# Alternating turns and unit products inside a score step of a two-layer attention trunk

## What is computed

```python
for l in range(DEPTH):                       # DEPTH = 2
    h = rms_norm(x, norm_g[l])
    proj = jnp.einsum('btd,dc->btc', h, w_in[l])
    q_a, kv_a, g_a, z_a, q_b, k_b, v_b, f_b, z_b, merge = jnp.split(proj, split_at, axis=-1)
    y_a = nsa_mixer(q_a, kv_a, g_a, ...) * jax.nn.silu(z_a)
    y_b = fox_mixer(q_b, k_b, v_b, f_b, b_forget[l]) * jax.nn.silu(z_b)
    merged = (jax.nn.sigmoid(r_a) * jnp.einsum('btc,cd->btd', y_a, w_proj_nsa[l])
              + jax.nn.sigmoid(r_b) * jnp.einsum('btc,cd->btd', y_b, w_proj_fox[l]))
    x = x + jnp.einsum('btd,de->bte', merged, w_out[l])
```

## Time and profile before

| | us |
|---|---|
| median of 3 runs | 1454.97 (1454.9 to 1455.04) |
| span of the profiled execution | 1452.2 |
| TensorE busy in it | 1443.0 (99%) |
| DVE, ACT, POOL busy | 1050.6, 915.4, 469.1 |
| attention of the two layers, about | 72 to 515 and 788 to 1230 |
| one inner cycle | 56.1 |

### The profile page before, as it was taken

One profiled execution on the slowest core, in us unless ns is written; L12 is line 12 of the kernel. 1 busy time (PEld: TensorE's weight loads), 2 busy tenths in 40 slices (PEclk: granted clock), 3 DMA queues, 4 the chain that ended last, 5 costly groups with the idle time before them and its releaser, 6 DMA issues.

```text
span 1452.2 us, 24707 instructions
## 1 busy us (share of the span) xinstructions
PE 1443.0 (99%) x7550; PEld 1223.2 (84%) x7550; DVE 1050.6 (72%) x2422; ACT 915.4 (63%) x1904; POOL 469.1 (32%) x578
## 2 busy tenths in 40 slices
PE   9999999999999999999999999999999999999998
PEld 7888888888888888888888888888888888888887
DVE  6888888888888864444578888888888887643444
ACT  6677777777877752223365877877877876522234
POOL 2435535445445310000023345445445453000000
PEclk9999999999999999999999999999999999999999
DMA  9221222222222143333453222222222212433332
GB/s 285 75 69 49 59 58 58 59 56 51 55 58 59 46 144 97 91 101 93 110 183 83 57 54 59 58 59 59 59 58 55 61 44 59 145 95 102 92 102 91
DMA packets 213890, 117.97 MB, mean 81 GB/s; under 512 B 9304, under 2 KB 212272, under 8 KB 213296
## 3 DMA queue, kind: packets, MB, share of 16 engines
q1 hardware_dynamic: 211408, 107.49, 27.2%
q0 software_dynamic: 1728, 8.66, 1.6%
q10 hardware_dynamic: 672, 0.83, 0.2%
HBM read 110.54 MB, written 6.42 MB: 81 GB/s over the span
## 4 chain that ended last, share of the span: by engine, by line
PE 98%; DVE 1%; issue 0%; ACT 0%; POOL 0%; DVEq 0%; POOLq 0%; ACTq 0%
PE acc L1814 69%; PE turned L1889 8%; PE o_pair L1914 7%; PE scores L1874 4%; PE scores L1876 4%; PE turned L2056 1%; PE misc L1933 1%; PE o_pair L1922 1%; PE scores L1814 1%; PE misc L1837 1%; PE o_pair L1948 1%; PE acc L2171 0%; PE o_pair L2171 0%; PE o_pair L2073 0%; PE scores L1992 0%
## 5 line engine op out<-in xcount | busy, mean ns | idle before, releaser
L1814 PE MATMUL acc<-u_hi,w_hi 128*128 128x512 f32 x1096 | 433.4, 395 | 0.0
L1814 PE MATMUL acc<-u_lo,w_hi 128*128 128x512 f32 x1096 | 430.9, 393 | 0.0
L1814 PE MATMUL acc<-u_hi,w_lo 128*128 128x512 f32 x1096 | 428.3, 393 | 0.0
L936 ACT ACTIVATE prob<-prob,row_max 128x384 f32<-128x384 f32 (+3 forms) x384 | 215.5, 561 | 143.2 <-DVE row_max L1400 140.8
L1217 DVE TENSOR_TENSOR w_lo<-w_raw,w_hi 128x1024 fp32r<-128x1024 f32 x184 | 230.7, 1254 | 83.1 <-ACT w_hi L807 82.4
L730 POOL TENSOR_SCALAR prob<-prob,row_inv,gates 128x256 f32<-128x256 f32 (+3 forms) x256 | 168.2, 657 | 302.8 <-DVE row_inv L1407 302.0
L807 ACT ACTIVATE w_hi<-w_raw 128x1024 fp32r<-128x1024 f32 x184 | 193.6, 1053 | 87.7 <-PE acc L1814 82.9
L1814 PEld LDWEIGHTS acc<-u_hi,w_hi 128*128 128x128 f32 x1096 | 206.4, 188 | 39.1 <-issue 0.2
L1814 PEld LDWEIGHTS acc<-u_lo,w_hi 128*128 128x128 f32 x1096 | 206.0, 188 | 37.0 <-issue 0.2
L1814 PEld LDWEIGHTS acc<-u_hi,w_lo 128*128 128x128 f32 x1096 | 206.4, 188 | 36.3
L1400 DVE CUSTOM_DVE_ANT_0 prob<-scores,causal 128x384 f32<-128x384 f32 (+3 forms) x384 | 185.7, 484 | 45.0 <-PE scores L1876 34.1
(11 more groups left out here) (276 smaller groups left out, 2346.1 us busy)
## 6 DMA issues: line engine op xcount, KB each, us to landing
w_raw<-in_w_in_dram SPq DMA_DIRECT2D x140, 512.0 KB, 3.7
w_raw<-in_w_proj_nsa_dram SPq DMA_DIRECT2D x16, 512.0 KB, 3.6
w_raw<-in_w_proj_fox_dram SPq DMA_DIRECT2D x16, 512.0 KB, 3.6
w_raw<-in_w_out_dram SPq DMA_DIRECT2D x16, 512.0 KB, 3.7
x_scratch<-xT POOLq DMA_DIRECT2D x2, 2048.0 KB, 9.2
xT<-x_scratch POOLq DMA_DIRECT2D x2, 2048.0 KB, 8.3
x_nat<-in_x_dram SPq DMA_DIRECT2D x4, 512.0 KB, 6.7
c_w<-in_cmp_w_k_dram SPq DMA_DIRECT2D x4, 512.0 KB, 6.1
```

What stands on the lines that cost most here:

```text
L936: act.activation(prob[:, ring, 0:width], prob[:, ring, 0:width], ACT.Exp, bias=row_max[:, ring:ring + 1], scale=-1.0, accum_out=row_sum[:, ...
L1814: ins = pe.matmul((bank or acc[par])[0:width, :], own_w, rhs, start=(n == 0), stop=(n == 23))
```

## The change

Between two turns of a step one product of the unit that is running is issued, if the slot still has one to issue. Where a narrow value product stands behind the first turn already, none is put there. The number of products at the end of each slot stays as it was.

```diff
-                def turn_step(pair, s, scored=None, ended=None):
+                def turn_step(pair, s, scored=None, ended=None, between=None):
...
                         if kt == 0 and ended:
                             value_narrow(*ended, 1)
+                        elif kt < qt:
+                            between()
...
+                def one_unit_product():
+
+                    nonlocal done
+                    if done < (plan.cum[s] if s < plan.slots else done):
+                        u = done // 24
+                        unit_piece(done - 24 * u, done - 24 * u + 1, *cycle.unit(u), free=bank_read(cycle, u))
+                        done += 1
+
...
-                        turn_step(*cycle.step(s - LAG_TURN), scored=scored if narrow else None, ended=ended_at(s))
+                        turn_step(*cycle.step(s - LAG_TURN), scored=scored if narrow else None, ended=ended_at(s),
+                                  between=one_unit_product)
```

## The result

| | before | changed |
|---|---|---|
| median (lowest to highest), us | 1454.93 (1454.84 to 1455.04) | 1465.55 (1464.99 to 1465.79) |
| profiled execution: its time, its span, us | not recorded, 1452.2 | 1465.69, 1464.0 |

The ratio is 1.0075, with a 95% interval of 1.0063 to 1.0086: slower by 10.6 us. The forecast was 1464.9. The spans of the two profiled executions differ by 11.8, about 1 us more than the medians: before, the median lies 2.8 above the span of the profile, in the changed kernel 1.6. What follows takes distances within an execution, which don't depend on that.

What follows compares the result with a forecast made beforehand. TensorE, busy 1443.0 of 1452.2 us, was taken as the bound, so only instruction costs and its waits matter. Late last turn 8.3 plus small costs 1.6 gave 9.9 on the median 1454.97: 1464.9, range 1459 to 1470.

Steps and rivals of the forecast that it cites:

- Term 3: Slot 6, inner cycles: last turn 0.69 us late, passed through ACT's copy, q_fox and DVE to TensorE; 12 cycles, 8.3 us.
- It already waits: ... 0.13 of wait: Slot 10, kernel before: TensorE's turn already waits 0.13 us, read from weight loads 0.36 apart instead of 0.23.
- Terms 1 and 2: Alternation price on TensorE, 1.0 us over 512 products, plus products behind 128-column matmuls, 1.0 us; 1.6 kept.
- Term 2: Two slots a cycle: unit product directly behind a 128-column score product costs net 0.03 us, times 32, 1.0 us.
- The factor of 80%: Share kept of the two small TensorE costs, as part falls under waits in slots 6 to 10 and first/last cycles.
- Second chain: Rival: slot 20's 0.24 us margin fails, DVE and POOL delay TensorE's turn; 3.2 us more, 1468 to 1471; chance 0.12.
- Swallowed: Rival: inner cycles' slot 10 is held by DVE's own load, so the 0.69 us never reaches TensorE; 1456.6; chance 0.14.
- Loads get hidden: Rival: grouped turns are bound by weight loads that products between them hide; 26 us saved, 1437; chance 0.04.

Runs made afterwards that it cites:

- split_only6: Changed kernel with products between turns only in slot 6 of the 12 inner cycles, and q_fox issued in two pieces in inner cycles; 1455.36 us.
- lead3: Changed kernel without alternation; in slot 6 of the 12 inner cycles three unit products stand ahead of the four grouped turns; 1462.28 us.
- scores3: Changed kernel without alternation; in slot 6 of the 12 inner cycles three unit products stand behind the turns, ahead of the scores; 1455.26 us.
- split_before: Kernel before the change, with q_fox issued in two pieces in inner cycles; no alternation; 1454.63 us.
- only6: Changed kernel with products between turns in slot 6 of the 12 inner cycles alone, 36 products; 1462.41 us.
- skip6: Changed kernel without its 36 products between turns in slot 6 of the 12 inner cycles; 1457.89 us.

## Why the prediction was right, and where not

**Time, sign and mechanism were right.** 9.9 us were forecast and 10.6 measured. The sizes of two terms were off, in opposite directions.

**Term 3, the late last turn (8.3).** Each link stands in the profile after: ACT's copy 0.70 late against the mark, DVE's idle time before q_fox unchanged, POOL's scaling ahead of slot 9 at 259.08-248.49 = 10.59 instead of 255.90-246.01 = 9.89, and the waits of slots 9 and 10. split_only6 shows q_fox to be the link, lead3 the late turn to be the cause, scores3 that the scores have no part. One step was mis-sized. "It already waits: ... 0.13 of wait" was read from the distance of weight loads; by the ends of matmuls there was no wait, and split_before freed none. In the distance of loads slot 10 did grow as forecast, from 0.36 to 0.50, but the first part of that still cost nothing. So slot 10 gives 0.10 and slot 9 0.53 (0.56 were forecast), in all 0.62 to 0.64 a cycle instead of 0.69; 12 cycles make 7.4 to 7.7, and only6 measured 7.2.

**Terms 1 and 2 (1.6 kept).** skip6 measured 2.7. The alternation, taken at 0.002 us, is 0.004 by the ends of matmuls and 0.006 if all of skip6's loss is put on it. That lies inside the bound of 0 to 0.01 that the rows had left, at another point than the one chosen. Term 2 stands at its place with the forecast 0.03 and isn't seen in the total. The factor of 80% was too low: it took part of this to vanish in first and last cycles, but skip6 lengthens a first cycle by 0.21 (56.30 to 56.51), as much as an inner one. Between slots 6 and 10 little vanishes: the change waits 0.62 a cycle where only6 waits 0.64.

**The rest.** The two errors, about 1 us each, have opposite signs and nearly cancel. That the forecast came closer than its terms is luck. First cycles grew by 0.21 to 0.24 and last ones by 0.16 to 0.18, where 0.2 was the bound. The inner cycle was to take 56.8 to 56.9 and takes 57.00. Its 308 matmuls are 312 in the trace, before and after; nothing rests on that.

**Second chain.** It held: the five inner cycles of the changed kernel have no wait outside slots 9 and 10. ACT in slot 20, POOL ahead of slot 0, and the turn's weight load, answering to the earlier trace rows:

```profile
286.80 0.49 ACT L945 ACTIVATE pt_hi<-turned 128x384 fp32r<-128x384 f32 x1 [0.69 <-PE turned L1889]
...
293.34 3.22 POOL L727 TENSOR_SCALAR prob<-prob,row_inv 128x384 f32<-128x384 f32 x2
...
295.26 0.14 PEld L1889 LDWEIGHTS turned<-ident,prob 128*128 128x128 f32 x1
```

The first of the two scalings, 1.69 us long in the earlier trace rows, ends at about 295.03, 0.23 ahead of the load; before it was 0.29. The margin lost 0.06, not the 0.23 by which that turn is late. The rows of ACT behind the copy show where the rest went. Before, then after:

```profile
283.79 1.06 ACT L807 ACTIVATE w_hi<-w_raw 128x1024 fp32r<-128x1024 f32 x1
```

```profile
287.19 1.05 ACT L807 ACTIVATE w_hi<-w_raw 128x1024 fp32r<-128x1024 f32 x1
```

Against the marks (246.01 and 248.49) the copy starts 1.06 later, w_hi 0.92, POOL's scaling 0.91 and the load 0.85. The copy is thus 0.21 late against the load, and 0.14 of it is taken up right behind the copy: before, w_hi started 0.04 after the copy had ended (283.26+0.49 = 283.75), in the changed kernel it starts 0.10 ahead of that end (286.80+0.49 = 287.29). The prediction had counted only the gap ahead of the load as cover.

**Swallowed** would have been 1456.6; DVE stayed full from q_fox to pt_lo. **Loads get hidden** is refuted as a gain: skip6, with nearly all the alternation and without the wait, is slower than before and not 26 us faster, and lead3, with its turns in a group, takes the same time as only6. The Trainium skill, page "TensorE: Matmul & The Clock Gate", section "LDWEIGHTS (loading the stationary operand)", gives a load of P columns P/1.2 ns, an estimate of 107 ns for 128 columns, which would suit a group bound by loads. The rows have a turn end 0.10 to 0.11 behind its predecessor even where that is a product, behind which its load is hidden (0.14 us long, from 252.58 on, under the product of 252.48 to 252.96), so by them the load does not set it. This rests on ends that the profile models. The sum of turn and product, 0.34 in a group and a run as in alternation, can't tell it from a load that is hidden by one product and shows again ahead of the next.

## What to carry to other kernels

Before a piece of work is put ahead of an instruction that signals, find who takes that signal the moment it comes: an engine that starts 0.04 us behind it, with a long undivided piece queued next and a full engine after that, passed on all but some 0.05 us of the delay here. Splitting the long piece (split_only6) took away nearly all of a 7 us loss, and the count of moved products said little about the price, their place nearly all. Read waits of TensorE from the ends of matmuls and check them against the length of the cycle; a late weight load alone is no lost time.

## What was not expected of the hardware

A weight load may come late for free. Behind a 512-column matmul the load of a 128-column turn stood 0.36 us behind its predecessor in the kernel before and 0.24 in split_before, and the turns ended 0.22 behind that matmul in both. It cost time when the gap was 0.50 (262.37-261.87 in the changed kernel: 0.10 lost). Against 0.24, lateness of 0.12 was free and lateness of 0.26 lost 0.10. The same page of the Trainium skill, section "Step-by-step: what each phase is for", says that the next tile's weights load while the present matmul runs; the trace agrees (the load at 262.37 lies within the product of 262.10 to 262.49), and adds how late such a load may start here.

The granted clock of TensorE was 1.00 in the window of the earlier trace rows and in the one that answers to it, its upper level (2.4 GHz), and on average 0.999 to 1.000 over the whole of each of the twelve profiles, so no step above rests on a change of clock.
